# Half of a gate column ahead of the drive products, and the first gate column's store behind the inputs' return, in the state-space stage of a Trainium2 kernel

## The reference

```python
h = rms_norm(x, pre_g)
conv_in, z_c, u_s, z_s, g_c, g_s = split(h @ w_in)        # 2048, 1024, 512, 512, 1024, 1024 columns
cu = silu(layer_norm(causal_conv31(ca * sigmoid(cb))))     # ca, cb: the halves of conv_in
conv_out = (cu * silu(z_c)) @ w_conv_out
# state space, 32 groups of 16 channels, 64 complex states each:
#   s_t = Abar s_{t-1} + Bbar u_t ;  y_t = Re(C s_t) + D u_t
y = gelu(s5_mimo(u_s)); y = y * sigmoid(y @ w_glu + b)
ssm_out = (y * silu(z_s)) @ w_ssm_out
out = (sigmoid(g_c) * conv_out + sigmoid(g_s) * ssm_out) @ w_out
return x + rms_norm(out, post_g)
```

## Time and profile before

| What | Value |
|---|---|
| Median of 3 runs | 2165.67 us (2165.45 to 2166.63) |
| The profiled execution, its own time | 2162.22 us |
| Its span, first to last instruction | 2160.5 us |
| PE busy | 2081.9 us (96% of the span) |
| DVE busy | 1360.8 us (63%) |
| ACT busy | 643.2 us (30%) |
| POOL busy | 216.1 us (10%) |
| Mean granted PE clock | 0.993 of full speed |

### The profile page before, as it was taken

One profiled execution on the slowest core, in us unless ns is written; L12 is line 12 of the kernel. 1 busy time (PEld: TensorE's weight loads), 2 busy tenths in 40 slices (PEclk: granted clock), 3 DMA queues, 4 the chain that ended last, 5 costly groups with the idle time before them and its releaser, 6 DMA issues. The chain is left out here.

```text
span 2160.5 us, 20801 instructions
## 1 busy us (share of the span) xinstructions
PE 2081.9 (96%) x6930; PEld 1065.1 (49%) x6930; DVE 1360.8 (63%) x1918; ACT 643.2 (30%) x1063; POOL 216.1 (10%) x180
## 2 busy tenths in 40 slices
PE   6999999999999999999899999999999999999998
PEld 5444444445556555556555445554444444444443
DVE  5787743364755746746742487528999997634633
ACT  4345521333433443434311521012321111241021
POOL 0000001112212212112000000001000000003200
PEclk8999999999999999999999999999999999999999
DMA  9333389321111111111320317269722222334021
GB/s 340 119 112 122 105 278 204 113 66 35 46 32 34 46 29 36 38 37 36 139 40 1 107 59 120 59 185 253 179 59 78 66 71 73 102 103 136 20 98 58
DMA packets 243824, 207.17 MB, mean 96 GB/s; under 512 B 52204, under 2 KB 202785, under 8 KB 243745
## 3 DMA queue, kind: packets, MB, share of 16 engines
q1 hardware_dynamic: 213393, 157.25, 24.5%
q0 software_dynamic: 13056, 42.99, 8.1%
q10 hardware_dynamic: 17312, 6.10, 1.3%
HBM read 182.55 MB, written 60.33 MB: 112 GB/s over the span
## 5 line engine op out<-in xcount | busy, mean ns | idle before, releaser
L2295 PE MATMUL bank<-hT,ring 128*128 128x512 f32 x576 | 254.2, 592 | 0.0
L2295 PE MATMUL bank<-resid,ring 128*128 128x512 f32 x432 | 191.3, 592 | 0.0
L2295 PEld LDWEIGHTS bank<-hT,ring 128*128 128x128 f32 x576 | 109.4, 190 | 137.8 <-issue 136.6
L1279 PE MATMUL bank<-hT,ring 128*128 128x512 f32 x336 | 157.7, 595 | 1.8 <-ACT silu_z L1515 1.8
L3205 DVE SCALAR_TENSOR_TENSOR yT<-s_arena,yT 128x1024 f32<-128x1024 f32 x120 | 153.0, 1275 | 0.0
L3205 DVE SCALAR_TENSOR_TENSOR s_arena<-s_arena 128x1024 f32<-128x1024 f32 x112 | 142.8, 1275 | 0.0
L2267 PE MATMUL bank<-hT,ring 128*128 128x512 f32 x320 | 139.4, 594 | 0.0
L2295 PEld LDWEIGHTS bank<-resid,ring 128*128 128x128 f32 x432 | 82.1, 190 | 103.3 <-issue 102.6
L1869 DVE SCALAR_TENSOR_TENSOR memory<-memory,col_exp_last,bank 128x128 f32<-128x128 f32 x64 | 22.2, 347 | 153.9 <-PE bank L1459 153.9
L2267 PEld LDWEIGHTS bank<-hT,ring 128*128 128x128 f32 x320 | 60.1, 190 | 73.7 <-issue 73.5
L2340 PE MATMUL bank<-ssm_y,ring 128*128 128x512 f32 x192 | 83.4, 592 | 0.0
(11 more groups left out here) (586 smaller groups left out, 3671.3 us busy)
## 6 DMA issues: line engine op xcount, KB each, us to landing
ada<-in_ada_w SPq DMA_DIRECT2D x8, 2048.0 KB, 8.1
ring<-in_gdn_in_w SPq DMA_DIRECT2D x32, 512.0 KB, 4.2
ring<-in_w_in SPq DMA_DIRECT2D x54, 256.0 KB, 2.9
ab_U_sums<-in_w_in POOLq DMA_DIRECT2D x6, 2048.0 KB, 19.9
resid<-in_x SPq DMA_DIRECT2D x8, 1024.0 KB, 8.9
ring<-in_lru_in_w SPq DMA_DIRECT2D x16, 512.0 KB, 3.9
ring<-ab_U_sums SPq DMA_DIRECT2D x32, 256.0 KB, 3.0
lru_arena<-in_ada_w SPq DMA_DIRECT2D x6, 1024.0 KB, 13.1
```

The lines of the kernel that those rows point to most:

```text
L1279: last = nc.tensor.matmul(bank[:, to, :], w[:, k, :], v[:, k, :], start=(first and k == 0), stop=(k == KB - 1), skip_group_check=not only)
L2295: last = nc.tensor.matmul(bank[:, to, :], w[:, k, :], src[:, k, :], start=(start and k == 0), stop=(k == HK - 1), skip_group_check=not alone)
```

## The change

Two things move; nothing is added to the work or taken from it.

On PE, the first half of gate column zc3 moves from behind drive(0) to ahead of it, and with it goes the wait for zc3's weights. On ACT, the store of gate column zc0 to memory moves from right behind its SiLU to behind ACT's four transfers of the inputs' return. For that the store becomes a function of its own, `keep_silu`, which `silu_c` still calls for every other column.

```diff
                     finish(early("zc2"))
                     act_b.wait(pe, "B1")
+                    tile = early("zc3")
+                    next(tile)
                     pe.wait_ge(u_loaded, BLK // 2 * 16)
                     pe.wait_ge(u_loaded_act, BLK // 2 * 16)
                     drive(0)
-                    finish(early("zc3"))
+                    finish(tile)
                     tile = early("zc4")
                     next(tile)
                     dve_b.wait(pe, "s0")
@@
                         act_b.mark(act.activation(silu_zc[:, n, :], pair(PAIR[f"zc{n}"]), ACT.Silu), f"zc{n}")
+                        if n:
+                            keep_silu(n)
+
+                    def keep_silu(n):
                         act_b.wait(act, f"zc{n}")
                         act.dma_start(zc_dram[n], silu_zc[:, n, :]).then_inc(zc_kept if n < 6 else zc_kept_late, 16)
@@
                         act.dma_start(u_blk[(BLK - 1 - t) * GH:(BLK - t) * GH, :, :],
                                       u_dram.rearrange("(g h) t k -> t h g k", h=GH)[t]).then_inc(u_loaded_act, 16)
+                    keep_silu(0)
                     silu_c(1)
```

## The result

The changed kernel is slower, as forecast. Its median is 2175.99 us over 11 runs (2169.22 to 2184.13), that of the kernel before 2163.47 over its 11. The ratio is 1.0056, with a 95% interval from 1.0045 to 1.0067, which is +12.1 us (+9.7 to +14.5). The forecast was +9.0 us, and 2174.7 us for the median. The profiled execution has a span of 2176.8 us against 2160.5, so 16.3 more.

What follows compares the result with a forecast made beforehand. PE, busy 96% of the span, bounds the kernel, so only its idle time can pay. Later read_out(0), 1376.31 against 1369.03, gives +7.28 us; with 1.73 of low clock +9.0, so 2174.7 us for the median, range 2169.2 to 2178.3.

Steps and rivals of the forecast that it cites:

- PE's idle time ahead of the half column: Before zc3's first half, PE waits 5.6 us for zc3's weights instead of 4.08 us for the inputs.
- Half column with low clock: zc3's first half ahead of drive(0): 7.06 us with its hand-over, plus 1.73 us for the low clock after the wait.
- DVE chain and start of read_out(0): Between drive(0)'s end and read_out(0): DVE's work up to `s0` takes 19.21 us, and PE starts 0.09 us later.
- PE's idle time ahead of read_out(0): PE waits about 5.4 us for DVE's `s0`, because only 13.87 us of PE work cover the 19.21 us chain.
- Low clock behind it: In read_out(0), after the 5.4 us wait, the clock is low again, costing 1.73 us, within 0 to 3.4.
- Everything behind absorbs: PE's stream behind read_out(0) is unchanged, and nothing there would absorb a delay.
- the rival of the store's second place: zc0's store takes 2.6 us of the DMA engines beside the return's end and zc3's weights: +11.6 us; chance 0.10.
- The rival of a small loss: The store's removal gives its full 1.75 us and neither idle time lowers the clock: +5.5, possibly under 4.3; chance 0.05.
- The second stall: Ahead of read_out(0): cover shrinks from 20.80 to 13.87 us against DVE's 19.21, so PE waits about 5.4 us.
- The weights behind the inputs: Ahead of drive(0): zc3's weights land at 1344.48, 1.5 us after the inputs and 5.5 after PE runs out of work.
- The store: Moving zc0's store behind ACT's part of the return: taken as 0, with -1.75 and +2.6 us as the ends.
- The second clock term: Low clock in read_out(0) after the wait for `s0`: 1.73 us, within 0 to 3.4.

Runs made afterwards that it cites:

- The longer cover: Full change, with the rest of zc3 and all of zc4 behind drive(0) and half of zc5 ahead of drive(1); ratio 1.0012 to the kernel before, +2.6 us.
- the early weights: Full change, with zc3's weights loaded ahead of zc2's into a free part of resid; ratio 1.0056 to the kernel before, +12.1 us.

## Why the prediction was right

By its own steps, with the first profile of the changed kernel:

| Step | Forecast | Measured |
|---|---|---|
| PE's idle time ahead of the half column | 5.6 us | 4.43 (again: 5.58) |
| Half column with low clock | 8.79 | 8.80 |
| drive(0) | 3.65, no idle time in front | 3.67, none |
| DVE chain and start of read_out(0) | 19.30 | 19.25 |
| PE's idle time ahead of read_out(0) | 5.4 | 5.34 |
| Low clock behind it | +1.73 | +8.9 (again: about +2.7 in read_out(0)) |
| Everything behind absorbs | nothing | nothing |

**The number** is less right than the steps. The measured +12.1 us lies inside the range by only half a microsecond (its end was +12.6), and above the +5.5 to +11 to which the prediction gave 0.74. It lies next to the +11.6 of the rival of the store's second place, but that isn't what happened: for that rival PE would have waited 5.6 + 2.6 = 8.2 us for the weights, and it waited 4.43 and 5.58. That the time came within 1.3 us of the forecast, 2175.99 against 2174.7, is partly luck: the forecast stood on the 2165.67 us of 3 runs, and over 11 the kernel before has 2163.47. One side sum was wrong as well. The rival of a small loss, "neither idle time lowers the clock", was put at 7.28 - 1.75 = +5.5, but the 7.28 holds 1.73 us of low clock in the half column, so it comes to +3.8. The forecast doesn't use it.

**The second stall** is the main step, and was right to a tenth: the cover of 13.87 us against a chain of 19.21. The longer cover removes it and with it most of the loss; the early weights leave it, and the loss stays.

**The weights behind the inputs** were right as the first thing waited for. Their wait of 4.43 and 5.58 us replaced the inputs' 4.08, so this step costs little by itself; what it does is to take the gain away. Only without it and without the second stall did the half column pay.

**The store** I set at 0, between -1.75 and +2.6. At the issues it is a gain: the eight K_lift issues take 11.48, 10.80, 10.83, 11.34 and 11.55 us in the five profiles with the store in its old place, and 9.37 to 10.55 in the nine with the store behind the return, 1.4 us less in the mean. PE's wait for zc3's weights was 4.43, 5.58, 2.37, 6.17 and 3.20 us in five profiles with the store moved, 4.35 in the mean, against 5.76 in the one without; the spread is wider than the difference, so 1.4 us is its size at the issues, and a gain at the landing isn't shown. The rule of the Trainium skill (DMA: Bandwidth & Descriptors, Queues, rings and completion order) that queues take turns, a packet at a time, was taken to put the weights up to 2.6 us later; the 2.6 is an estimate of the prediction, from its rows. The mean of the five shows no such lag; the 6.17 us of one of them lie in its direction. No run here shows the turns themselves.

**The second clock term** is what was mis-sized: 1.73 us by the drive(0) row, with 3.4 as its upper end. In the first profile it is read_out(0) with 18.45 - 10.19 = 8.3 us and the half column behind it with 7.73 - 7.06 = 0.7, and in the five profiles with this stall in front of read_out(0) the low clock lasted 20.5, 6.8, 10.2, 6.8 and 20.5 us. I took the length from a stretch where the clock came back after 3.4 us, and carried it to another stretch of other work. In the changed kernel's two profiles the term is 7.2 and 1.0 us above its 1.73, 4.1 in the mean, and the steps in front of drive(0) give back 0.6. That leaves 3.5 us above the forecast, near the 3.1 of the timed runs. It is also one reason, beside the landing of the weights, why the changed kernel's runs spread over 15 us and those of the kernel before, over as many runs, over 6. What sets the length stays open.

## What to carry to other kernels

Before work is moved in front of a wait to fill it, two sums are due: what that work needs itself, and when it lands (here, in the kernel before, its weights came 1.5 us behind the very inputs whose wait it was to fill), and what it covered where it stood (here 19.2 us of DVE, of which it took away 7 where only 1.4 were to spare). A filler is free only if both come out; otherwise bring its inputs forward and take the cover from the work behind, which together made the stage 5.8 us shorter than before (4.1 and 5.8 us in the timed runs). And a stall of 5 us in front of a long run of small matmuls can cost more in clock than in waiting: 8.9 against 5.3 us in one execution here, 2.7 against 5.3 in another.

## What the runs showed of the hardware

- The same idle time of PE, 5.3 us, was followed by 6.8 us of low clock in some executions and 20.5 in others, of one and the same kernel. Behind shorter idle times it fell in some and not in others: after 3.20, 4.08 and 4.11 us it fell, after 2.37, 2.73 and 3.5 us it did not. After each of 4.43 us and more in these stages it fell.
- One 512 KB load behind the inputs on its queue took 16.0 us from issue to landing in one execution and 19.7 in another of the same kernel (PE waited 2.37 us for it once, 6.17 the other time).
